# A float32 decoder trunk on one core: the high and the low moving part side by side in one 512-wide matmul, and outer weight sums made by adding transfers

## The chip, the cores and the metric

The kernel runs on one core of a Trainium2 chip. The metric is the device time of one execution in microseconds (us), with all inputs in the chip's main memory at the start and the output there at the end. Five engines work side by side, each through its own list of instructions, and wait for each other through semaphores: TensorE (PE, matmuls; its weight loads are listed as PEld), VectorE (DVE), ScalarE (ACT), GpSimd (POOL), and SyncE (SP), which issues most transfers.

## The reference

Two layers act on x of 512 tokens by 1024 features. Each layer is a feed-forward block, a token mixer (gated linear attention in layer 0, causal window means in layer 1), a cross-attention to a memory of 256 tokens, and a second feed-forward block. All is float32. What matters here are the four feed-forward blocks:

```python
def swiglu_ffn(h, w_gu, w_down):
    g, u = jnp.split(h @ w_gu, 2, axis=-1)
    return (jax.nn.silu(g) * u) @ w_down

for i in range(DEPTH):                                   # DEPTH = 2
    x = x + 0.5 * swiglu_ffn(rmsnorm(x, n_ffn1[i]), ffn1_w_gu[i], ffn1_w_down[i])
    ...                                                  # mixer, cross-attention
    x = x + 0.5 * swiglu_ffn(rmsnorm(x, n_ffn2[i]), ffn2_w_gu[i], ffn2_w_down[i])
```

`w_gu` is 1024 by 5632 (gate and up columns, 2816 each), `w_down` is 2816 by 1024.

## The kernel before

**Split numbers.** A float32 operand is split into a high and a low part. ACT writes the high part (`hi_part`, a copy to fp32r, L1388), DVE the low part (`lo_part`, value minus high part, L2055). One product then takes three matmuls: weights high times moving high, weights high times moving low, weights low times moving high. In the plain stages these are L418 to L420, 512 tokens wide.

**Slots and runs.** Gate and up are computed in 22 column blocks of 128 for each feed-forward block n = 0 to 3. The first 4, 2, 2 and 2 blocks are plain. The other 78 are "mixed slots". They come in eight runs, named (n, part): part 0 has 7, 9, 9 and 9 slots, part 1 has 11 each. Behind each run comes half of the down projection (`half_down`, or `down_by_token` for n = 3), with its own weights in the same buffers.

**A mixed slot** computes a 2 by 2 block product with seven products in place of eight. The weights of a slot have four quarters (first or second 512 rows; gate or up), the moving side has four as well (first or second 512 features; "low" tokens 0 to 255 or "high" tokens 256 to 511). PE makes the products in the order P1, P5, P6, P4, P2, P7, P3 (`mixed_slot`, L1013), where P4 still belongs to the slot before. Some use a quarter as it is, others a sum of quarters. Each product is four blocks of 128 rows by three 256-wide matmuls (`block_product`, L1000, matmuls at L1007 to L1009), 84 matmuls in a slot. P1 and P2 go to PSUM bank 6, P5 to bank 7, P6, P7 and P4 to one of two banks that alternate from slot to slot, P3 to bank d.

**Sums of weights.** DVE makes four sums for the next slot: two "outer" ones in one instruction (`sum_columns`, L2087, 1024 elements in each partition), and two more (`sum_three`, L2091; `sum_four`, L2101). Then each of the seven weight operands ("forms") is split by ACT (`form_hi`) and DVE (`form_lo`). A form may be written only when the product that used its buffer in the running slot is done.

**Behind the products.** ACT copies P1 from bank 6 into the alternating bank (L1487; its semaphore step is SEEDED, and PE's P6 waits for it), so that P6, P7 and P4 add to it. It moves P5 to SBUF (`sq`). DVE forms the fourth start value in bank d (`seed_fourth`, L2164), and then gate times norm, silu (ACT) and gate times up, for low and high tokens (L2172 to L2196, each 256 wide). Last come the split of the result (`half_hi` by ACT, `half_lo` by DVE).

**What sets the order.** The order on each engine is written out by hand in the three functions `mixed_run` (ACT, L1448; DVE, L2153) and `mixed_slot` (PE). An engine executes its list in order, so what stands behind a waiting instruction waits as well. In the run (3, 0) DVE also transposes a block of x in each slot (`turn_block`, L2427).

**Transfers.** SP loads each slot's weights in two transfers of 512 KB (`load_ffn`, L521), two slots ahead of use. POOL adds squares and issues a few transfers of its own.

Of the kernel before, what the change touches and what calls it, by code (L numbers as in the profile page):

```python
# [41 lines left out]
def trunk(nc, io, out):  # L42
# [153 lines left out]
    with ctx:  # L196
# [74 lines left out]
        s_hi, s_lo = region("s_hi", 0, [P, 4, KH, TH], F32R), region("s_lo", 16 * KB, [P, 4, KH, TH], F32R)  # L271
        w_sums = region("w_sums", 32 * KB, [P, 4, KH, P])
# [86 lines left out]
        names = """first_loaded first_cols_done vec_loaded gates_loaded identity_ready consts_ready mask_ready  # L359
# [14 lines left out]
                y_gained y_out_by_dve y_out_by_act stored  # L374
# [4 lines left out]
                mixed_act_step mixed_dve_step x_half_ready"""  # L379
# [106 lines left out]
        def _(sp):  # L486
# [33 lines left out]

            def load_ffn(n):  # L521
# [2540 lines left out]
```

## Time and profile before

| | us |
|---|---|
| median of 3 runs (1935.63 to 1936.52) | 1935.84 |
| the profiled execution, its own time | 1936.11 |
| its span, from the first to the last instruction | 1934.4 |
| PE busy | 1925.1 |
| DVE busy | 1410.6 |
| ACT busy | 964.2 |
| mean granted TensorE clock | 0.999 |

Spans and busy times come from the one profiled execution. A busy time counts an instruction from its start to its modelled end. Instructions of one engine overlap by their ends, so the distance between two starts tells how long one really holds its engine. The profiled execution took 1.7 us more than its span.

### The profile page before, as it was taken

The numbers are of one execution on the slowest core, as the hardware profiler recorded it, in microseconds if no ns is written. First come the engines' busy times: TensorE is split into PE (matmuls) and PEld (weight loads), VectorE is DVE, ScalarE is ACT, GpSimd is POOL, SyncE is SP. The second block draws the span as 40 slices with busy tenths as digits, with TensorE's granted clock in tenths as the row PEclk, the third lists the DMA queues.
The fourth block names the chain that finished last, engine by engine and source line by source line (L and its number), as shares of the span: only waits on it lengthen the run. The fifth ranks groups of instructions, "written<-read, shape, count | busy, mean of one in ns | idle before, by whom it ended". The sixth has DMA issues, their size and how long they took to land.

```text
span 1934.4 us, 31412 instructions
## 1 busy us (share of the span) xinstructions
PE 1925.1 (100%) x12020; PEld 1741.1 (90%) x12020; DVE 1410.6 (73%) x2173; ACT 964.2 (50%) x1612; POOL 168.6 (9%) x207
## 2 busy tenths in 40 slices
PE   9999999999999999999999999999999999999998
PEld 7998998888898889989998998999888889989997
DVE  7865985687765659947976995698487569937964
ACT  7542554355554546524644653355356446524543
POOL 2000002100112120000001000000312121200000
PEclk9999999999999999999999999999999999999999
DMA  6333334323433634333334333333353424343332
GB/s 181 87 104 103 109 93 136 108 66 109 131 127 114 174 87 110 103 103 109 101 91 120 91 100 94 101 109 104 112 180 116 109 74 116 109 159 109 109 98 87
DMA packets 285894, 215.01 MB, mean 111 GB/s; under 512 B 15347, under 2 KB 268401, under 8 KB 285793
## 3 DMA queue, kind: packets, MB, share of 16 engines
q1 hardware_dynamic: 270112, 192.96, 33.5%
q0 software_dynamic: 6752, 18.68, 3.7%
q10 hardware_dynamic: 8928, 2.11, 0.5%
q8 instruction: 54, 0.88, 0.2%
q14 instruction: 48, 0.39, 0.1%
HBM read 203.23 MB, written 10.49 MB: 110 GB/s over the span
## 4 chain that ended last, share of the span: by engine, by line
PE 96%; DVE 2%; ACT 1%; issue 1%; POOL 0%; DMA 0%; ACTq 0%; DVEq 0%; POOLq 0%
PE ps L418 18%; PE ps L420 18%; PE ps L419 18%; PE ps L1007 13%; PE ps L1009 13%; PE ps L1008 13%; DVE w_lo L2055 1%; ACT w_hi L1388 1%; POOL mem_scratch L721 0%; PE ps L933 0%; PE ps L867 0%; DVE sums L2808 0%; DMA x_tok<-in_x 0%; DVE sums L2828 0%; DVE up L2997 0%
## 5 line engine op out<-in xcount | busy, mean ns | idle before, releaser
L2055 DVE TENSOR_TENSOR w_lo<-raw,w_hi 128x512 fp32r<-128x512 f32 (+5 forms) x367 | 403.2, 1099 | 258.0 <-ACT w_hi L1388 257.3
L1388 ACT ACTIVATE w_hi<-raw 128x512 fp32r<-128x512 f32 (+5 forms) x367 | 341.5, 948 | 267.1 <-PE ps L420 254.9
L1007 PE MATMUL ps<-s_hi,w_hi 128*128 128x256 f32 x1248 | 353.8, 283 | 0.1
L1009 PE MATMUL ps<-s_hi,w_lo 128*128 128x256 f32 x1248 | 353.2, 283 | 0.0
L1008 PE MATMUL ps<-s_lo,w_hi 128*128 128x256 f32 x1248 | 353.2, 283 | 0.0
L1008 PE MATMUL ps<-h_lo,w_hi 128*128 128x256 f32 x936 | 264.9, 283 | 0.0
L1009 PE MATMUL ps<-h_hi,w_lo 128*128 128x256 f32 x936 | 264.9, 283 | 0.0
L1007 PE MATMUL ps<-h_hi,w_hi 128*128 128x256 f32 x936 | 264.8, 283 | 0.0
L1388 ACT ACTIVATE w_hi<-w_sums 128x512 fp32r<-128x512 f32 x312 | 187.5, 625 | 138.4 <-DVE w_sums L2087 69.4
L1007 PEld LDWEIGHTS ps<-s_hi,w_hi 128*128 128x128 f32 x1248 | 239.5, 192 | 0.9 <-issue 0.5
L1009 PEld LDWEIGHTS ps<-s_hi,w_lo 128*128 128x128 f32 x1248 | 239.5, 192 | 0.0
L1008 PEld LDWEIGHTS ps<-s_lo,w_hi 128*128 128x128 f32 x1248 | 239.5, 192 | 0.0
L2055 DVE TENSOR_TENSOR w_lo<-w_sums,w_hi 128x512 fp32r<-128x512 f32 x312 | 211.4, 681 | 0.0
L418 PE MATMUL ps<-half_hi,w_hi 128*128 128x512 f32 x528 | 205.7, 390 | 0.6 <-DVE w_lo L2055 0.6
L419 PE MATMUL ps<-half_lo,w_hi 128*128 128x512 f32 x528 | 205.5, 389 | 0.0
L420 PE MATMUL ps<-half_hi,w_lo 128*128 128x512 f32 x528 | 205.4, 389 | 0.0
L418 PE MATMUL ps<-h_hi,w_hi 128*128 128x512 f32 (+1 forms) x480 | 182.0, 379 | 0.5 <-DVE w_lo L2055 0.5
L419 PE MATMUL ps<-h_lo,w_hi 128*128 128x512 f32 (+1 forms) x480 | 180.2, 375 | 0.0
L420 PE MATMUL ps<-h_hi,w_lo 128*128 128x512 f32 (+1 forms) x480 | 180.1, 375 | 0.0
L1008 PEld LDWEIGHTS ps<-h_lo,w_hi 128*128 128x128 f32 x936 | 179.6, 192 | 0.3
L1007 PEld LDWEIGHTS ps<-h_hi,w_hi 128*128 128x128 f32 x936 | 179.6, 192 | 0.3
L1009 PEld LDWEIGHTS ps<-h_hi,w_lo 128*128 128x128 f32 x936 | 179.6, 192 | 0.0
(396 smaller groups left out, 3438.1 us busy)
## 6 DMA issues: line engine op xcount, KB each, us to landing
raw<-in_ffn_w_gu SPq DMA_DIRECT2D x172, 512.0 KB, 5.0
raw<-in_ffn_w_down SPq DMA_DIRECT2D x36, 768.0 KB, 4.4
raw<-in_x_w_kv SPq DMA_DIRECT2D x16, 1024.0 KB, 5.8
raw<-in_ffn_w_down SPq DMA_DIRECT2D x24, 640.0 KB, 4.2
raw<-in_gla_w_in SPq DMA_DIRECT2D x12, 1024.0 KB, 5.2
raw<-in_x_w_q SPq DMA_DIRECT2D x8, 1024.0 KB, 5.1
raw<-in_x_w_o SPq DMA_DIRECT2D x8, 1024.0 KB, 6.0
raw<-in_gla_w_out SPq DMA_DIRECT2D x8, 512.0 KB, 3.4
```

The source lines that it names most:

```text
L418: nc.tensor.matmul(out_ap, left[0], right[0], start=first, stop=False)
L419: nc.tensor.matmul(out_ap, left[0], right[1], start=False, stop=False)
L420: return nc.tensor.matmul(out_ap, left[1], right[0], start=False, stop=last)
L1007: nc.tensor.matmul(to, hi[:, kk, :], right_hi, start=fresh, stop=False, skip_group_check=True)
L1008: nc.tensor.matmul(to, hi[:, kk, :], right_lo, start=False, stop=False, skip_group_check=True)
L1009: last = nc.tensor.matmul(to, lo[:, kk, :], right_hi, start=False, stop=kk == KH - 1, skip_group_check=True)
L1388: return nc.scalar.activation(out_ap, in_ap, ACT.Copy, **kw)
L2055: return nc.vector.tensor_tensor(out_ap, value, hi.bitcast(F32), ALU.subtract)
```

## The change

**Moving parts side by side.** `h_hi` and `h_lo` become the two halves of `h_both`, `s_hi` and `s_lo` those of `s_both`. In six of the seven products (all but P5) one 512-wide matmul takes the high and the low part together: its left 256 columns of PSUM hold weights high times moving high, its right 256 columns weights high times moving low. The third matmul (weights low times moving high) adds to the left half as before. So a product has 8 matmuls in place of 12, and its value is the sum of the two halves of its bank. Adding these halves is new work of ACT (`up_right`, `high_right`, `low_right` take right halves to SBUF, a copy with scale -1 carries one to bank d, and the copy of P1 is 512 wide) and of DVE (`up_sum`, `high_sum`, `low_sum`, `up_part` with `up_ready`).

**Outer sums by transfer.** From the third slot of each run on (62 of the 78 slots) SP loads one quarter for each outer sum (256 KB each) two slots ahead. POOL then issues a transfer that adds the other quarter onto it (`accum_op=ALU.add`). DVE's `sum_columns` is then only a wait. The signs of sums on both sides are changed so that an addition serves.

**Cut diff** (the rest of it renames counters and semaphores):

```diff
@@ SP
+            def load_outer(m, both, s):
+
+                before, sums = 16 * transfers_before(m), outer_sums[in_run[m] % 2]
+                for g, (loaded_sem, opened, last_form) in enumerate(((sig.t1_loaded, OPENED, P5),
+                                                                     (sig.t3_loaded, 0, P7))):
+                    sp.wait_ge(*form_lo_count(m - 2, last_form))
+                    sp.wait_ge(loaded_sem, opened + before)
+                    sp.dma_start(sums[:, g], both[:, 0:KH, g, s * P:(s + 1) * P]).then_inc(loaded_sem, 16)
...
+                        if w in mixed_slots and by_transfer(mixed_slots.index(w)):
+                            load_outer(mixed_slots.index(w), both, s)
+                            sp.wait_ge(sig.w_lo_ready, w - 1)
+                            sp.dma_start(raw[:, w % 2, :, 0:P], both[:, :, 0, s * P:(s + 1) * P])\
+                              .then_inc(raw_loaded[w % 2], 16)
+                            sp.dma_start(raw[:, w % 2, KH:, P:], both[:, KH:, 1, s * P:(s + 1) * P])\
+                              .then_inc(raw_loaded[w % 2], 16)
+                            continue
@@ POOL
+            def add_outer(n, part, l):
...
+                pool.wait_ge(sig.t1_loaded, OPENED + before + 16)
+                pool.wait_ge(sig.t1_added, T1_OPENED + before)
+                pool.dma_start(sums[:, 0], up[:, 0:KH, s * P:(s + 1) * P], accum_op=ALU.add).then_inc(sig.t1_added, 16)
@@ PE, block_product
-                    nc.tensor.matmul(to, hi[:, kk, :], right_hi, start=fresh, stop=False, skip_group_check=True)
-                    nc.tensor.matmul(to, hi[:, kk, :], right_lo, start=False, stop=False, skip_group_check=True)
-                    last = nc.tensor.matmul(to, lo[:, kk, :], right_hi, start=False, stop=kk == KH - 1,
+                    if i == P5:
+                        nc.tensor.matmul(to, hi[:, kk, :], right[:, 0, :], start=fresh, stop=False, skip_group_check=True)
+                        nc.tensor.matmul(to, hi[:, kk, :], right[:, 1, :], start=False, stop=False, skip_group_check=True)
+                    else:
+                        nc.tensor.matmul(ps[:, bank, :], hi[:, kk, :], right, start=fresh, stop=False,
+                                         skip_group_check=True)
+                    last = nc.tensor.matmul(to, lo[:, kk, :], right[:, 0, :], start=False, stop=kk == KH - 1,
@@ PE, last_block (P4 of a run's last slot)
-                pe.wait_ge(sig.mixed_dve_step, dve_step(end - 1, C22_READY))
+                pe.wait_ge(sig.mixed_dve_step, dve_step(end - 1, UP_READY))
@@ ACT, mixed_run
+                def up_right(m, s):
+                    act.wait_ge(sig.product_done, product_count(m, P3))
+                    act.wait_ge(sig.mixed_dve_step, dve_step(m, UP_READY))
+                    hi_part(sq[:, s % 2, TH:], ps[:, d, TH:]).then_inc(sig.mixed_act_step, 1)
...
+                    if l > 0:
+                        up_right(m - 1, s - 1)
+                        form_hi(m, P3, sig.product_done, product_count(m - 1, P3))
                     act.wait_ge(sig.product_done, product_count(m, P1))
...
-                    nc.scalar.activation(ps[:, banks[l % 2], 0:TH], ps[:, 6, 0:TH], ACT.Copy).then_inc(sig.mixed_act_step, 1)
-                    if l > 0:
-                        form_hi(m, P3, sig.product_done, product_count(m - 1, P3))
+                    nc.scalar.activation(ps[:, banks[l % 2], :], ps[:, 6, :], ACT.Copy).then_inc(sig.mixed_act_step, 1)
@@ DVE, mixed_run, the slots after the first
+                    up_sum(m - 1, s - 1)
+                    form_lo(m, P3)
+                    low_gated(m - 1, s - 1)
...
+                    high_sum(m - 1, s - 1, before)
                     form_lo(m, P4)
...
+                    high_rms(m - 1, s - 1)
+                    low_sum(m, s)
                     if following:
                         sum_four(m + 1)
...
+                    low_rms(m, s)
+                    high_gated(m - 1, s - 1)
                     if following:
                         form_lo(m + 1, P2)
...
+                    up_part(m, s, b)
+                    half_mid_lo(s - 1)
+                    up_ready(m, s, b)
+                    if following:
                         form_lo(m + 1, P7)
```

**ACT where one slot ends and the next begins**, in the middle of a run. In the rows, `sq<-ps 128x256` behind the P7 form is `up_right` (new), `w_hi<-raw` is the form of P3 and then that of P1, and `ps<-ps` is the copy of P1 for which PE's P6 waits. Before:

```order
L1388 ACTIVATE half_hi<-t 128x512 [waits mixed_dve_step]
L1388 ACTIVATE w_hi<-w_sums 128x512 [waits product_done,w_sum_ready]
L1487 ACTIVATE ps<-ps 128x256 [waits mixed_dve_step,product_done]
L1388 ACTIVATE w_hi<-raw 128x512 [waits product_done,raw_loaded_even]
L1388 ACTIVATE w_hi<-raw 128x512 [waits product_done,raw_loaded_odd]
L1388 ACTIVATE sq<-ps 128x256 [waits mixed_dve_step,product_done]
```

The same place, of the changed kernel:

```order
L1464 ACTIVATE half_hi<-t 128x512 [waits mixed_dve_step]
L1464 ACTIVATE w_hi<-outer_odd 128x512 [waits product_done,t3_added]
L1464 ACTIVATE sq<-ps 128x256 [waits mixed_dve_step,product_done]
L1464 ACTIVATE w_hi<-raw 128x512 [waits product_done,raw_loaded_odd]
L1586 ACTIVATE ps<-ps 128x512 [waits mixed_dve_step,product_done]
L1464 ACTIVATE w_hi<-raw 128x512 [waits product_done,raw_loaded_even]
L1464 ACTIVATE sq<-ps 128x256 [waits mixed_dve_step,product_done]
```

Two instructions now stand ahead of the copy `ps<-ps`: `up_right`, which waits for a step of DVE, and the form of P3, which stood behind it.

**DVE in the second half of a slot**, in the middle of a run, from the form of P4 to the last sum with bank d. L2179 (before) forms the up value of the high tokens, for which PE's P4 waits. Before:

```order
L2055 TENSOR_TENSOR w_lo<-w_sums,w_hi 128x512 [waits form_hi_ready]
L2196 TENSOR_TENSOR t<-t,sq 128x256 [waits mixed_dve_step,silu_done]
L2101 TENSOR_TENSOR w_sums<-raw,w_sums 128x512 [waits form_lo_ready,w_sum_ready]
L2172 TENSOR_TENSOR t<-ps,rms 128x256 [waits mid_ready,product_done]
L2055 TENSOR_TENSOR w_lo<-raw,w_hi 128x512 [waits form_hi_ready]
L2055 TENSOR_TENSOR half_lo<-t,half_hi 128x512 [waits mid_hi_ready]
L2179 TENSOR_TENSOR sq<-ps,sq 128x256 [waits mixed_dve_step,product_done]
```

The same place, of the changed kernel (L2297 `high_rms`, L2302 `low_sum`, L2214 `sum_four`, L2307 `low_rms`, L2313 `high_gated`, L2320 `up_part`, L2325 `up_ready`):

```order
L2163 TENSOR_TENSOR w_lo<-inner_sums,w_hi 128x512 [waits form_hi_ready]
L2297 TENSOR_TENSOR t<-t,rms 128x256 [waits mixed_dve_step]
L2302 TENSOR_TENSOR t<-t,ps 128x256 [waits mixed_act_step]
L2214 TENSOR_TENSOR inner_sums<-raw,inner_sums 128x512 [waits form_lo_ready,w_sum_ready]
L2307 TENSOR_TENSOR t<-t,rms 128x256 [waits mixed_dve_step]
L2313 TENSOR_TENSOR t<-t,sq 128x256 [waits mixed_dve_step,silu_done]
L2163 TENSOR_TENSOR w_lo<-raw,w_hi 128x512 [waits form_hi_ready]
L2320 SCALAR_TENSOR_TENSOR sq<-ps,sq 128x256 [waits mixed_dve_step,product_done]
L2163 TENSOR_TENSOR half_lo<-t,half_hi 128x512 [waits mid_hi_ready]
L2325 TENSOR_TENSOR sq<-sq,ps 128x256 [waits mixed_dve_step]
```

`up_ready` (L2325), for which ACT's `up_right` and PE's P4 wait, stands ten instructions behind the form of P4 and last.

**DVE in a run's last slot**, from the split of the down weights (1536 elements, L2055 or L2163) on. Before:

```order
L2055 TENSOR_TENSOR w_lo<-raw,w_hi 128x1536 [waits w_hi_ready]
L2190 TENSOR_TENSOR t<-ps,rms 128x256 [waits product_done]
L2055 TENSOR_TENSOR w_lo<-w_sums,w_hi 128x512 [waits form_hi_ready]
L2196 TENSOR_TENSOR t<-t,sq 128x256 [waits mixed_dve_step,silu_done]
L2172 TENSOR_TENSOR t<-ps,rms 128x256 [waits mid_ready,product_done]
L2179 TENSOR_TENSOR sq<-ps,sq 128x256 [waits mixed_dve_step,product_done]
L2055 TENSOR_TENSOR half_lo<-t,half_hi 128x512 [waits mid_hi_ready]
```

And of the changed kernel:

```order
L2163 TENSOR_TENSOR w_lo<-raw,w_hi 128x1536 [waits w_hi_ready]
L2292 TENSOR_TENSOR t<-t,ps 128x256 [waits mixed_act_step]
L2163 TENSOR_TENSOR w_lo<-inner_sums,w_hi 128x512 [waits form_hi_ready]
L2297 TENSOR_TENSOR t<-t,rms 128x256 [waits mixed_dve_step]
L2302 TENSOR_TENSOR t<-t,ps 128x256 [waits mixed_act_step]
L2307 TENSOR_TENSOR t<-t,rms 128x256 [waits mixed_dve_step]
L2313 TENSOR_TENSOR t<-t,sq 128x256 [waits mixed_dve_step,silu_done]
L2320 SCALAR_TENSOR_TENSOR sq<-ps,sq 128x256 [waits mixed_dve_step,product_done]
L2163 TENSOR_TENSOR half_lo<-t,half_hi 128x512 [waits mid_hi_ready]
L2325 TENSOR_TENSOR sq<-sq,ps 128x256 [waits mixed_dve_step]
```

The step for which the run's last P4 waits (L2179 before, L2325 now) moved from ahead of `half_lo` to behind it, and four more instructions stand in between.

## Rows read from the trace of the kernel before

**Rows 1.** The page: busy time by engine, then the chain that ended last.
```profile
PE 1925.1 (100%) x12020; PEld 1741.1 (90%) x12020; DVE 1410.6 (73%) x2173; ACT 964.2 (50%) x1612; POOL 168.6 (9%) x207
...
PE 96%; DVE 2%; ACT 1%; issue 1%; POOL 0%; DMA 0%; ACTq 0%; DVEq 0%; POOLq 0%
```

**Rows 2.** Groups by form: count, busy us, mean ns of one, idle before.
```profile
L2087 DVE TENSOR_TENSOR w_sums<-raw 128x1024 f32<-128x1024 f32 x78 | 98.3, 1260 | 0.0
...
L1487 ACT ACTIVATE ps<-ps 128x256 f32<-128x256 f32 x78 | 28.7, 368 | 62.9 <-PE ps L1009 62.9
...
L1388 ACT ACTIVATE xq_hi<-ps 128x512 fp32r<-128x512 f32 x16 | 9.6, 597 | 32.5 <-PE ps L420 32.4
```

**Rows 3.** Timeline, PE, 512-wide matmuls (start us, length us): 39 starts apart.
```profile
20.05 0.39 PE L420 MATMUL ps<-h_hi,w_lo 128*128 128x512 f32 x1
...
28.89 0.39 PE L420 MATMUL ps<-h_hi,w_lo 128*128 128x512 f32 x1
```

**Rows 4.** Timeline, ACT, one slot from copy of P1 to the next.
```profile
94.58 0.37 ACT L1487 ACTIVATE ps<-ps 128x256 f32<-128x256 f32 x1 [0.88 <-PE ps L1009]
...
104.66 0.37 ACT L1487 ACTIVATE ps<-ps 128x256 f32<-128x256 f32 x1 [0.88 <-PE ps L1009]
104.94 1.14 ACT L1388 ACTIVATE w_hi<-raw 128x512 fp32r<-128x512 f32 x2
```

**Rows 5.** Timeline, DVE, the middle of the same slot; in brackets, idle before.
```profile
103.28 0.69 DVE L2055 TENSOR_TENSOR half_lo<-t,half_hi 128x512 fp32r<-128x512 f32 x1 [0.41 <-ACT half_hi L1388]
103.89 0.41 DVE L2179 TENSOR_TENSOR sq<-ps,sq 128x256 f32<-128x256 f32 x1
104.23 0.68 DVE L2055 TENSOR_TENSOR w_lo<-w_sums,w_hi 128x512 fp32r<-128x512 f32 x1
104.83 0.41 DVE L2185 TENSOR_TENSOR t<-t,ps 128x256 f32<-128x256 f32 x1
105.59 0.69 DVE L2055 TENSOR_TENSOR w_lo<-raw,w_hi 128x512 fp32r<-128x512 f32 x1 [0.35 <-ACT w_hi L1388]
106.20 1.22 DVE L2087 TENSOR_TENSOR w_sums<-raw 128x1024 f32<-128x1024 f32 x1
107.34 0.69 DVE L2055 TENSOR_TENSOR w_lo<-raw,w_hi 128x512 fp32r<-128x512 f32 x1
```

**Rows 6.** Timelines, PE and DVE, where the run (0, 1) begins.
```profile
184.59 0.28 PE L1007 MATMUL ps<-h_hi,w_hi 128*128 128x256 f32 x1
...
187.34 1.22 DVE L2087 TENSOR_TENSOR w_sums<-raw 128x1024 f32<-128x1024 f32 x1
```

**Rows 7.** Timelines, ACT, DVE and PE, where the run (0, 1) ends.
```profile
288.52 1.49 ACT L1388 ACTIVATE w_hi<-raw 128x1536 fp32r<-128x1536 f32 x1 [1.11 <-PE ps L1009]
...
290.04 1.76 DVE L2055 TENSOR_TENSOR w_lo<-raw,w_hi 128x1536 fp32r<-128x1536 f32 x1 [1.14 <-ACT w_hi L1388]
291.72 0.42 DVE L2190 TENSOR_TENSOR t<-ps,rms 128x256 f32<-128x256 f32 x1
...
295.47 0.40 PE L418 MATMUL ps<-half_hi,w_hi 128*128 128x512 f32 x1
```

**Rows 8.** Timelines, run (3, 0): copies of P1, and P7 behind DVE's L2164.
```profile
1626.55 0.37 ACT L1487 ACTIVATE ps<-ps 128x256 f32<-128x256 f32 x1 [0.36 <-PE ps L1009]
...
1631.71 0.42 DVE L2164 TENSOR_TENSOR ps<-ps,sq 128x256 f32<-128x256 f32 x1
...
1632.25 0.19 PEld L1007 LDWEIGHTS ps<-s_hi,w_hi 128*128 128x128 f32 x1 [0.19 <-issue]
...
1632.47 0.28 PE L1008 MATMUL ps<-s_lo,w_hi 128*128 128x256 f32 x1
...
1687.97 0.37 ACT L1487 ACTIVATE ps<-ps 128x256 f32<-128x256 f32 x1 [0.38 <-PE ps L1009]
```

**Rows 9.** One slot by window: busy by engine, clock, DMA share, GB/s; then DMA issues.
```profile
82.30:92.38 10.08, 10.08 (x86) 10.08 (x86) 9.33 (x18) 6.00 (x13) 0.00 (x0) 1.00 0.38 104
...
p_tok<-p_scratch POOLq DMA_DIRECT2D x12, 256.0 KB, 3.5
```

More of the change, by code:

```diff
@@ L183, in mixed_end, with by_transfer, transfers_before, sum_count @@
         return mixed_first[n, part] + mixed_count(n, part)
+    def by_transfer(m):
+        return in_run[m] >= 2
+    def transfers_before(m):
+        return sum(by_transfer(i) for i in range(m))
+    def sum_count(m, step):
+        return OPENED + 3 * m - transfers_before(m) + step - int(by_transfer(m))
     def first_of_run(m):
@@ L723, in memory_store, with add_run @@
                             .then_inc(sig.mem_stored, 16)
+            def add_outer(n, part, l):
+                m, s = mixed_first[n, part] + l, l + (PLAIN_FIRST[n], HALF)[part]
+                before, sums = 16 * transfers_before(m), outer_sums[l % 2]
+                up = (io.ffn1_w_gu, io.ffn2_w_gu)[n % 2][n // 2].rearrange("(k p) (g n) -> p k g n", p=P, g=2)[:, :, 1, :]
+                pool.wait_ge(sig.t1_loaded, OPENED + before + 16)
+                pool.wait_ge(sig.t1_added, T1_OPENED + before)
+                pool.dma_start(sums[:, 0], up[:, 0:KH, s * P:(s + 1) * P], accum_op=ALU.add).then_inc(sig.t1_added, 16)
+                pool.wait_ge(sig.t3_loaded, before + 16)
+                pool.wait_ge(sig.t3_added, T3_OPENED + before)
+                pool.dma_start(sums[:, 1], up[:, KH:, s * P:(s + 1) * P], accum_op=ALU.add).then_inc(sig.t3_added, 16)
+            def add_run(n, part):
+                for l in range(2, mixed_count(n, part)):
+                    add_outer(n, part, l)
             row = 0
@@ L1407, in form_hi @@
                 w = mixed_slots[m]
-                if i in SUM_OF:
-                    act.wait_ge(sig.w_sum_ready, OPENED + 3 * m + SUM_STEP[i])
+                if i == P5 and by_transfer(m):
+                    act.wait_ge(sig.t1_added, T1_OPENED + 16 * (transfers_before(m) + 1))
+                elif i == P7 and by_transfer(m):
+                    act.wait_ge(sig.t3_added, T3_OPENED + 16 * (transfers_before(m) + 1))
+                elif i in SUM_OF:
+                    act.wait_ge(sig.w_sum_ready, sum_count(m, SUM_STEP[i]))
                 else:
@@ L1503, in mixed_run @@
                     else:
+                        high_right(m - 1, s - 1, banks[(l + 1) % 2])
                         form_hi(m, P4, sig.product_done, product_count(m, P4))
+                    low_right(m, s)
+                    if l > 0:
                         high_silu(m - 1, s - 1)
@@ L1515, in mixed_run @@
                         form_hi(m + 1, P7, sig.product_done, product_count(m, P7))
+                up_right(m, s)
                 split_hi((w + 1) % 2, area[w + 1], loaded[w + 1], product_count(m, P3), slot_rows[w + 1],
                          sig.product_done)
+                high_right(m, s, banks[(end - m0 - 1) % 2])
                 high_silu(m, s)
@@ new lines, in high_rms, with low_sum @@
+                def high_rms(m, s):
+                    dve.wait_ge(sig.mixed_dve_step, dve_step(m, HIGH_SUM))
+                    nc.vector.tensor_tensor(t[:, s % 2, TH:], t[:, s % 2, TH:], rms[:, TH:], ALU.mult)\
+                      .then_inc(sig.mixed_dve_step, 1)
+                def low_sum(m, s):
+                    dve.wait_ge(sig.mixed_act_step, act_step(m, LOW_RIGHT))
+                    nc.vector.tensor_tensor(t[:, s % 2, 0:TH], t[:, s % 2, 0:TH], ps[:, 6, 0:TH], ALU.add)\
+                      .then_inc(sig.mixed_dve_step, 1)
```

263 lines of the change are left out of this document (159 added, 104 removed).

## The prediction

> **What bounds the kernel now.** I read the page first: PE is busy for 1925.1 of 1934.4 us and is 96% of the chain that ended last [rows 1]. DVE, at 73%, looks free, but that share is a mean over stages, so I read one mixed slot by window and by timeline. There DVE is busy for 9.33 of 10.08 us [rows 9]. Its list waits in two places only, 0.41 us for ACT's `half_hi` and 0.35 us for the form of P3 [rows 5]. A slot lasts from one copy of P1 to the next, 104.66 - 94.58 = 10.08 us [rows 4], which is 84 matmuls of 0.120 us without a hole. So in a mixed slot PE is the bound and DVE is 0.8 us behind it. In the run (3, 0), where DVE has one more instruction in each slot, the distance is already (1687.97 - 1626.55) / 6 = 10.24 us, and P7 there sits behind DVE's L2164 [rows 8]. DVE is the next bound, and it is near.
>
> **Matmuls.** Thirty-nine starts of 512-wide matmuls span 28.89 - 20.05 = 8.84 us, 0.2267 us each [rows 3]. Two 256-wide ones cost 0.240 us [rows 4]. One in place of two saves 0.0133 us. There are 6 x 4 = 24 such pairs in a slot, and 78 slots [rows 2]: 1872 x 0.0133 = **25.0 us** less on PE. A slot of PE alone becomes 24 x (0.2267 + 0.120) + 12 x 0.120 = 9.76 us. No row shows a 512-wide matmul next to a 256-wide one; the saving lies between 0 and 0.0267 us a pair (0.240 less 512 columns at 2.4 GHz, 0.2133, the granted clock being 1.00 [rows 9]), and I take the rows' 0.0133. The Trainium skill, "TensorE: Matmul & The Clock Gate", section "Back-to-back issue gap", gives an isolated warm gap of N / 2.4 + 2.5 ns, so one matmul fewer would save 2.5 ns and the whole change 4.7 us. The rows show 13.3 ns over the columns at both widths, so here the measurement decides.
>
> **DVE's sum.** Distances between starts give 0.60 us for 512 elements, 0.335 for 256, 1.14 for the outer sums [rows 5]. Before, a slot holds 10 of 512, one outer sum and 6 of 256: 6.03 + 1.14 + 2.01 = 9.18 us. After, the outer sum goes (-1.14) and four more of 256 come (+1.34): 9.38 us of 9.76. It still fits, but with half the slack. ACT gets three to four more PSUM reads of 0.28 us, well inside its idle time (6.00 busy of 10.08 [rows 9]). So no engine is full, and the question is who waits for whom.
>
> **The new wait.** PE's P6 needs the copy of P1 (SEEDED). Before, that copy needed P1 alone: it ended 0.03 + 0.16 + 0.37 = 0.56 us behind P1 [rows 4], while P5 keeps PE busy for 1.44, so P6 had 0.9 us in hand. Now ACT must first do `up_right` of the slot before, which waits for DVE's `up_ready`, and then the form of P3. `up_ready` is the last of ten DVE instructions that start with the form of P4, and they wait for PE's P4. This is a closed round, from one end of P4 to the next:
> - PE to ACT 0.03, `high_right` 0.285, form of P4 0.62 to its end, ACT to DVE 0.03: 0.965 us;
> - DVE: form of P4, `sum_four`, form of P2, `half_lo` at 0.603, five of 256 at 0.335, and `up_ready` 0.416 to its end [rows 5]: 4.50;
> - DVE to ACT 0.03, `up_right` 0.285 (104.94 - 104.66 [rows 4]), form of P3 0.52 (two take 1.14 to the end of the second [rows 4]), the copy 0.58: 1.415;
> - PE's restart, P6 and P4: 0.19 + 2 x 1.387 + 0.163 (a product's modelled end lies that far behind its last matmul's 0.120): 3.127.
>
> The sum is **10.005 us**. PE alone would need 9.76, so each steady slot holds PE for 0.245 us. Two of these prices have no row of their own. The copy, 512 wide in PSUM, lies between 0.37 (the 256-wide one) and 0.74 (twice that); a 512-wide PSUM read takes 0.597 [rows 2], so 0.58. PE's restart: L2164 ended at 1632.13, the weights were loaded from 1632.25, and the second matmul started at 1632.47, as if the product had begun at 1632.35 [rows 8]: 0.22. The best case is 0.03, as between ACT and DVE; I take 0.19.
>
> **First slot of a run (8).** DVE begins its list 187.34 - 184.59 = 2.75 us behind PE [rows 6] and must still make an outer sum itself, since transfers begin with the third slot. Walking on: outer sum done 3.96, `seed_fourth` at 4.92 (behind ACT's scaled copy of P6), forms of P1 and P5 and `sum_three`, ACT's forms of P6 and P4, then `low_right`, and DVE's `low_sum` at 8.01. From there 0.603 x 4 + 0.335 x 3 + 0.416 = 3.83 us to the end of `up_ready`, 11.84; + 1.42 for ACT and 0.19 for the restart = 13.45. PE could start the second slot's P6 at 11.44. Wait: **2.0 us**. Before, P1 of the second slot follows without a hole; now it also waits 0.24 us for `low_sum`.
>
> **Last slot (8).** P4 of the last slot now waits for `up_ready` behind DVE's split of the down weights and behind `half_lo`. From the slot's start: P6 ends at 4.62 (with its 0.245 hold), + 0.03, scaled copy 0.285, ACT's split 1.49, + 0.03 = 6.46; DVE's split 1.67 (291.72 - 290.04 [rows 7]), form of P4 0.603, six of 256 at 0.335 with one gap of 0.11 = 10.85; `half_lo` waits for ACT until 11.27; + 0.60 + 0.416 = 12.29; restart 12.48. PE is free at 10.0. Wait: **2.48 us**. Before, P4 ran through and down began at 295.47 without a hole [rows 7]. Down has all its inputs in time afterwards: its fifth weight block comes only 8.2 us in.
>
> **The sum.** 8 x 0.24 + 8 x 2.0 + 62 x 0.245 + 8 x 2.48 = 1.9 + 16.0 + 15.2 + 19.8 = 52.9 us of holes, + 0.6 for the third slot of the run (3, 0), where the transposes stand in the way, - 25.0 of matmuls, - 1.6 of the holes that this run has already. That is **+26.9 us**. The profiled execution took 1936.1 us, 0.3 above the median: **1963 us**.
>
> **At no cost:** the loads and the adding transfers. A load starts when DVE has split the same form two slots back, and its sum is split some 17 us later (two slots less the forms between). The load of 256 KB takes about 3.5 us [rows 9]; no adding transfer is in the trace, so I bound it by 3.5 and three times that. In the worse case 3 us are left. POOL is idle in the runs, and its later work (squares) starts after them. If the cover fails: rival 3.
>
> **Rivals.**
> 1. *PE stays the bound* (faster). The round would have to close in 9.76 us and the ends of a run without a hole; the former needs the copy at 0.37, the latter 4 us less of DVE work. With all holes gone: 1936.1 - 25.0 - 1.6 = 1910 us. Against it: the lists of DVE and ACT. At the favourable ends together (copy 0.37, pairs saving 0.0267) the same walk still gives +8 us, 1944.
> 2. *Holes and gain cancel* (within 0.2%): the holes at half, 26 us.
> 3. *Adds come late.* A slot now moves 1.8 MB in place of 1.0. With the DMA share 0.38 at 104 GB/s [rows 9] that is 0.66 of the slot if an add costs a load, 0.84 at twice, and the bound from three times on. At four times a slot takes 12.3 us, 2.3 more in each of 62: 1963 + 143 = 2106 us. Nothing speaks for it but the lack of a row.
> 4. *DVE or ACT slower by 5%*, from the doubled traffic or from PSUM reads beside 512-wide writes: each round grows by 0.25 us, 1979 us.
> 5. *The clock falls after the holes.* All stretches read 1.00 [rows 9], but none has such holes. Sixteen holes of 2 us, each followed by 2 us of work at 1.2 GHz in place of 2.4: + 16 us, 1979 us.
>
> **How the numbers follow.** Forecast 0.68 (1944 to 1978, by copy, restart and pair price); rivals: 1 has 0.08, 2 has 0.05, 3 has 0.05, 4 has 0.08, 5 has 0.06. The range 1944 to 1988 holds the forecast and rivals 4 and 5, 0.82. A measurement of this kernel can tell about 0.2%, 4 us, from no change: faster 0.08, same 0.05, slower 0.87.
>
> **What would show it.** Right: matmul starts 0.227 and 0.120 us apart in pairs; PE idle before P6 of each slot, released by ACT's copy, 0.2 to 0.3 us in the middle of runs and 2 us in the second slot; 2.5 us ahead of each run's last P4, released by DVE's L2325; copies of P1 10.0 us apart. Wrong: no idle time of PE before P6, or copies 9.8 us apart (rival 1); ACT or DVE waiting for t1_added or t3_added (3); DVE's 512-wide distance above 0.61 us (4); a granted clock below 0.99 (5).

## The result

The changed kernel takes 1989.5 us (median of 4 runs, 1981.5 to 1992.1) beside 1936.0 for the kernel before (4 runs, 1935.6 to 1936.5): ratio 1.0269, 95% interval 1.0255 to 1.0283. The forecast was 1963, its range 1944 to 1988. The direction was right; the loss is +53.5 us where +27 were forecast. The profiled execution took 1989.0 us, with a span of 1987.3 (1936.1 and 1934.4 before).

The page of the changed kernel, the lines that answer to [rows 1]: busy time by engine, the chain that ended last, and the adding transfers (count, KB each, median us from issue to landing).

```profile
PE 1944.0 (98%) x10148; PEld 1657.3 (83%) x10148; DVE 1456.4 (73%) x2423; ACT 1073.3 (54%) x1924; POOL 328.9 (17%) x331
...
PE 84%; DVE 9%; ACT 4%; issue 3%; DMA 0%; ACTq 0%; DVEq 0%
...
outer_even<-in_ffn_w_gu POOLq DMA_DIRECT2D x70, 256.0 KB, 4.8
```

PE has 1872 matmuls fewer and is busy 19 us longer. Its share of the chain fell from 96 to 84%. The two largest waits of PE (total us, times, longest):

```profile
PE ps L1083 <- DVE sq L2325: 17.7, 8, 2.3
PE ps L1083 <- ACT ps L1586: 15.9, 8, 2.1
```

Eight waits of 2.2 to 2.3 us for `up_ready` at the ends of the runs and eight of 2.0 to 2.1 for the copy of P1 in the second slots: both are the forecast's. But they are 33.6 us, not the whole loss. The rest is in what follows them. This is PE where the second slot of the run (0, 0) has its hole (timeline), then the same stretch and the next by window (PE busy first, then PEld, DVE, ACT, POOL; the granted clock is the third number from the end).

```profile
65.15 0.28 PE L1085 MATMUL ps<-s_both,w_lo 128*128 128x256 f32 x1
67.42 0.50 PE L1083 MATMUL ps<-s_both,w_hi 128*128 128x512 f32 x1 [1.99 <-ACT ps L1586]
67.75 0.28 PE L1085 MATMUL ps<-s_both,w_lo 128*128 128x256 f32 x1
...
68.22 0.61 PE L1083 MATMUL ps<-s_both,w_hi 128*128 128x512 f32 x1
68.63 0.41 PE L1085 MATMUL ps<-s_both,w_lo 128*128 128x256 f32 x1
68.84 0.63 PE L1083 MATMUL ps<-s_both,w_hi 128*128 128x512 f32 x1
...
71.75 0.28 PE L1085 MATMUL ps<-h_both,w_lo 128*128 128x256 f32 x1
71.86 0.40 PE L1083 MATMUL ps<-h_both,w_hi 128*128 128x512 f32 x1
```

```profile
66.00:68.00 2.00, 0.58 (x3) 0.54 (x4) 2.00 (x5) 2.00 (x5) 0.18 (x1) 1.00 0.51 60
68.00:70.00 2.00, 2.00 (x9) 1.66 (x8) 2.00 (x5) 0.98 (x3) 0.00 (x0) 0.56 1.01 200
70.00:72.00 2.00, 2.00 (x9) 1.77 (x8) 1.25 (x3) 0.63 (x2) 0.87 (x1) 0.59 1.10 314
72.00:74.00 2.00, 2.00 (x14) 1.72 (x13) 1.42 (x4) 1.29 (x3) 0.40 (x1) 1.00 1.15 252
```

From 68.2 to 71.7 a 512-wide matmul takes some 0.43 us to the next start and a 256-wide one 0.21, about twice the usual 0.23 and 0.12. The granted clock fell from 1.00 to 0.50 (2.4 to 1.2 GHz) 0.8 us after PE had begun again. Read in half microseconds it stays there for 3.41 us, which loses 1.71 us. Eleven of the sixteen holes have such a fall behind them: four second slots and seven run ends. None is in the trace of before while PE still has work.

To see where the 52.9 us between the two profiled executions lie I summed the starts of the first P5 matmul of each slot, over the eight runs:

| us | before | changed | difference | forecast |
|---|---|---|---|---|
| first P1 of the runs | 11.5 | 11.2 | -0.3 | -0.4 |
| first slots | 69.1 | 69.4 | +0.3 | -0.2 |
| second slots | 81.0 | 102.8 | +21.8 | +13.4 |
| the 54 slots between | 545.3 | 545.4 | +0.2 | -5.1 |
| last slots, to the start of down | 80.6 | 102.9 | +22.3 | +19.2 |
| all outside the runs | 1146.9 | 1155.5 | +8.6 | 0 |

The forecast's column is its own terms divided up (26.9 in all; its +0.6 and -1.6 for the run (3, 0) stand with the slots between). The +8.6 is mostly the end falls that reach into down: a run's last P4 lasts 1.4 us, the slow stretch 3.4. In e1_filled below, which has no fall, this row is 1146.8 again.

### The profile page after: what moved, and what is told of

Read it like the earlier page. It is cut to its first block, busy times and chain, and to the rows that moved or that the text cites. A ratio compares the mean times of both kernels' runs of the same rounds, so it can differ in the third digit from the quotient of the medians.

```text
span 1987.3 us, 28928 instructions
## 1 busy us (share of the span) xinstructions
PE 1944.0 (98%) x10148; PEld 1657.3 (83%) x10148; DVE 1456.4 (73%) x2423; ACT 1073.3 (54%) x1924; POOL 328.9 (17%) x331
## 4 chain that ended last, share of the span: by engine, by line
PE 84%; DVE 9%; ACT 4%; issue 3%; DMA 0%; ACTq 0%; DVEq 0%
PE ps L1083 19%; PE ps L442 17%; PE ps L443 16%; PE ps L444 16%; PE ps L1085 11%; DVE w_lo L2163 3%; ACT w_hi L1464 2%; PE ps L1081 2%; PE ps L1080 2%; DVE s_both L2163 0%; DVE half_lo L2163 0%; DVE outer_odd L2197 0%; DVE t L2302 0%; DMA raw<-in_x_w_kv 0%; DVE t L2307 0%
## 5 line engine op out<-in xcount | busy, mean ns | idle before, releaser
L2163 DVE TENSOR_TENSOR w_lo<-raw,w_hi 128x512 fp32r<-128x512 f32 (+5 forms) x367 | 402.9, 1098 | 254.7 <-ACT w_hi L1464 245.3
L1083 PE MATMUL ps<-s_both,w_hi 128*128 128x512 f32 x936 | 346.5, 408 | 16.4 <-ACT ps L1586 15.9
L1083 PE MATMUL ps<-h_both,w_hi 128*128 128x512 f32 x936 | 343.7, 404 | 17.7 <-DVE sq L2325 17.7
L1085 PE MATMUL ps<-s_both,w_lo 128*128 128x256 f32 x1248 | 352.2, 282 | 0.0
L1085 PE MATMUL ps<-h_both,w_lo 128*128 128x256 f32 x936 | 265.5, 284 | 0.0
L1085 PEld LDWEIGHTS ps<-s_both,w_lo 128*128 128x128 f32 x1248 | 237.3, 190 | 0.0
L1083 PEld LDWEIGHTS ps<-h_both,w_hi 128*128 128x128 f32 x936 | 178.6, 191 | 64.8 <-issue 20.0
L1083 PEld LDWEIGHTS ps<-s_both,w_hi 128*128 128x128 f32 x936 | 176.7, 189 | 66.7 <-ACT ps L1586 20.5
L442 PE MATMUL ps<-h_both,w_hi 128*128 128x512 f32 (+1 forms) x480 | 182.0, 379 | 0.8 <-DVE w_lo L2163 0.8
L443 PE MATMUL ps<-h_both,w_hi 128*128 128x512 f32 (+1 forms) x480 | 180.2, 375 | 0.0
L444 PE MATMUL ps<-h_both,w_lo 128*128 128x512 f32 (+1 forms) x480 | 180.1, 375 | 0.0
L1085 PEld LDWEIGHTS ps<-h_both,w_lo 128*128 128x128 f32 x936 | 179.6, 192 | 0.3
L2163 DVE TENSOR_TENSOR w_lo<-inner_sums,w_hi 128x512 fp32r<-128x512 f32 x156 | 107.0, 686 | 6.2
L442 PEld LDWEIGHTS ps<-h_both,w_hi 128*128 128x128 f32 x480 | 90.4, 188 | 16.8 <-DVE w_lo L2163 1.2
```

The source lines that it names most:

```text
L442: nc.tensor.matmul(out_ap, left[0], right[0], start=first, stop=False)
L443: nc.tensor.matmul(out_ap, left[0], right[1], start=False, stop=False)
L444: return nc.tensor.matmul(out_ap, left[1], right[0], start=False, stop=last)
L1083: nc.tensor.matmul(ps[:, bank, :], hi[:, kk, :], right, start=fresh, stop=False, skip_group_check=True)
L1085: last = nc.tensor.matmul(to, lo[:, kk, :], right[:, 0, :], start=False, stop=kk == KH - 1, skip_group_check=True)
L2163: return nc.vector.tensor_tensor(out_ap, value, hi.bitcast(F32), ALU.subtract)
```

## The steady slot, term by term

One round of ACT and DVE in the steady state (timelines, ACT and DVE, then PE), for [rows 4, 5]:

```profile
92.26 0.38 ACT L1464 ACTIVATE t<-ps 128x256 f32<-128x256 f32 x1 [0.50 <-PE ps L1085]
92.54 0.62 ACT L1464 ACTIVATE w_hi<-inner_sums 128x512 fp32r<-128x512 f32 x1
...
93.20 0.69 DVE L2163 TENSOR_TENSOR w_lo<-inner_sums,w_hi 128x512 fp32r<-128x512 f32 x1
...
97.28 0.41 DVE L2325 TENSOR_TENSOR sq<-sq,ps 128x256 f32<-128x256 f32 x1
...
97.79 0.39 ACT L1464 ACTIVATE sq<-ps 128x256 f32<-128x256 f32 x1 [0.77 <-DVE sq L2325]
98.07 0.62 ACT L1464 ACTIVATE w_hi<-raw 128x512 fp32r<-128x512 f32 x1
98.59 0.59 ACT L1586 ACTIVATE ps<-ps 128x512 f32<-128x512 f32 x1
...
99.23 0.51 PE L1083 MATMUL ps<-s_both,w_hi 128*128 128x512 f32 x1
99.58 0.28 PE L1085 MATMUL ps<-s_both,w_lo 128*128 128x256 f32 x1
```

From `high_right` to DVE's form of P4: 93.20 - 92.26 = 0.94 (forecast 0.935). DVE's list: 4.08 + 0.41 = 4.49 (4.50). The copy's end behind `up_right`'s start: 99.18 - 97.79 = 1.39 (1.385). Only DVE to ACT took 97.79 - 97.69 = 0.10 where 0.03 was put in, and the way from the copy's end to the next `high_right` 3.18 in place of 3.16. The round is 10.10 us instead of 10.005; the copies of P1 are 10.10 apart, those of before 10.08 [rows 4]. Little of the wait shows as idle time: P6 starts 0.20 us behind P5's last matmul (99.03 in the same timeline) where 0.12 is usual, and its first wide matmul holds PE for 99.58 - 99.23 = 0.35 us in place of 0.23. The two make up the 0.19 us by which a slot is longer than the 9.91 of PE alone (below).

## The experiments

The kernel before ran beside each group of experiments; its median was 1936.2 to 1936.4 us each time, so times of different groups can be compared. Three edits of order, A, B and C, come back in several kernels.

**Is it idle time that lets the clock fall?** The kernel e1_filled keeps every wait and gives PE something to do ahead of it:

```diff
+            def fill(n, part, times):
...
+                for _ in range(times):
+                    nc.tensor.matmul(ps[:, (o + 3) % 4, :], h_both[:, 0, 0, 0:P], h_both[:, :, 0, 0:TH], ...)
...
                 form_ready(P6)
+                if l == 1 and j is None:
+                    fill(n, part, 8)
                 pe.wait_ge(sig.mixed_act_step, ...)
```

(and `fill(n, part, 9)` ahead of the waits of `last_block`). The kernel also writes out the second and third slots of a run in PE's list instead of looping over them; no run has that alone.

> The changed kernel; before its wait for the copy of P1 in the second slot of each run TensorE does 8 extra 512-wide matmuls, and before its wait ahead of the run's last P4 it does 9 more, all into a PSUM bank that nobody reads (8 x 0.227 = 1.8 us of a hole of 2.13, 9 x 0.227 = 2.0 us of one of 2.35). The first two slots behind the first are written out instead of looped. The waits stay, so no hole closes; only TensorE is not idle in it. Theory (the clock falls because TensorE was idle, 11 times in the profiled execution of the changed kernel, 1.71 us lost each time): granted clock 0.999, no matmuls at 0.43 us spacing, time 1989.5 - 11 x 1.71 = 1971 us. Rival (the clock falls for another cause, the wide matmuls or the doubled traffic, and its place behind the holes is chance): clock 0.99 as before the fill, 1982 to 1992 us.

Measured: 1972.3 us (4 runs, 1971.9 to 1972.5), mean clock 1.0. PE and the windows in the same place:

```profile
65.54 0.28 PE L1085 MATMUL ps<-s_both,w_lo 128*128 128x256 f32 x1
65.66 2.00 PE L1093 MATMUL ps<-h_both 128*128 128x512 f32 x8
67.72 0.50 PE L1083 MATMUL ps<-s_both,w_hi 128*128 128x512 f32 x1
...
68.00:70.00 2.00, 2.00 (x13) 1.74 (x13) 2.00 (x5) 1.48 (x5) 0.00 (x0) 1.00 1.08 174
```

P6 starts 67.72 - 65.54 = 2.18 us behind P5's last matmul, nearly as long as the hole was (2.27), so the wait is all there; the granted clock is 1.00 from 7.4 us to behind PE's last matmul. More work in the same holes makes the kernel 17.2 us faster, ten falls' worth. The spread of the runs goes from 10.6 to 0.6 us: it was the falls that varied (of the changed kernel's runs the shortest, 1981.5 us, had a mean clock of 0.995, the longest, 1992.1, one of 0.988). The rival (wide matmuls or traffic) is out, since both are still there. They are so in e5_both_orders too, which has loops as the changed kernel has, no such holes, and no fall either.

> As e1_filled, with 4 extra matmuls ahead of each of the 16 waits in place of 8 and 9: 0.9 us of work, then 1.2 to 1.5 us idle. Theory (shorter idle stretches leave the clock alone, as the eight of 1.42 us in e3_ready_first did): granted clock 0.999, no matmuls at 0.43 us spacing, 1972 us as with the full fill, all runs within 1 us. Rival (any idle stretch of over a microsecond can let it fall): some falls, 1975 to 1985 us, runs some us apart.

Measured: 1973.6 us (1973.5 to 1973.9), no fall. The waits that are left:

```profile
PE ps L1083 <- DVE sq L2337: 10.5, 8, 1.4
PE ps L1083 <- ACT ps L1598: 8.4, 9, 1.1
```

With 1.0 to 1.4 us idle in place of 2.0 to 2.3, none of the 16 waits let the clock fall.

> The changed kernel once more, unaltered, for its clock falls. Theory (16 waits of 2.1 to 2.4 us lie where the clock can fall, and which of them it falls behind is not set by the program): 1.71 us each, another set of waits than the 11 of the first profile, runs spread over 1980 to 1993 us in line with their mean granted clocks. Rival (fixed places: the second slots of a layer's second part never, the others always): the same 11, 1989 us.

Measured: 1988.1 us (1986.5 to 1991.0). Again 11 falls, but another set: the holes ending at 1026.53 and 1124.76, whose counterparts had a fall in the first profile, have none, and those ending at 1816.78 and 1918.62 have one. Windows of two of them, behind the second slots of two runs:

```profile
1124.00:1126.00 2.00, 1.24 (x7) 1.11 (x8) 2.00 (x5) 2.00 (x5) 0.00 (x0) 1.00 1.11 147
1126.00:1128.00 2.00, 2.00 (x13) 1.72 (x12) 2.00 (x5) 1.16 (x4) 0.00 (x0) 1.00 0.80 210
...
1816.00:1818.00 2.00, 1.22 (x3) 1.04 (x4) 1.74 (x5) 2.00 (x5) 0.27 (x1) 0.66 0.36 90
1818.00:1820.00 2.00, 2.00 (x8) 1.70 (x7) 1.27 (x3) 0.32 (x2) 0.39 (x1) 0.50 1.30 201
```

The rival of fixed places is out. What decides which of the holes of 2.0 to 2.3 us lets the clock fall stays open. e8_no_transfers (below) has the same sixteen holes and six falls.

**B: the copy of P1 first.** It stands on ACT ahead of `up_right` and the form of P3:

```diff
-        ACT_ORDER = (UP_RIGHT, SEEDED, P5_TAKEN,
+        ACT_ORDER = (SEEDED, UP_RIGHT, P5_TAKEN,
...
-                    if l > 0:
-                        up_right(m - 1, s - 1)
-                        form_hi(m, P3, sig.product_done, product_count(m - 1, P3))
                     act.wait_ge(sig.product_done, product_count(m, P1))
...
                     nc.scalar.activation(ps[:, banks[l % 2], :], ps[:, 6, :], ACT.Copy).then_inc(sig.mixed_act_step, 1)
+                    if l > 0:
+                        up_right(m - 1, s - 1)
+                        form_hi(m, P3, sig.product_done, product_count(m - 1, P3))
```

> The changed kernel with one order changed on ScalarE: in each slot the 512-wide copy of P1 stands ahead of up_right and the form of P3 instead of behind them. Theory (the holes before P6 are this order): no idle time before P6; second slot 2.13 us shorter in 8 runs (-17.0) and 4 clock falls fewer (-6.8), 62 steady slots 9.91 us (24 pairs x 0.353 + 12 x 0.120) in place of 10.10 (-11.8); the waits ahead of the last P4 stay at about 2.35 us: 1989.5 - 35.6 = 1954 us. Rival (VectorE is then the bound, since up_right comes 0.5 us later and VectorE's up_sum waits for it): steady slots 10.0 to 10.2 us, VectorE's idle time in front of up_sum, 1960 to 1972 us.

Measured: 1961.0 us (1960.6 to 1962.9). Steady slots (ACT's copies of P1), then PE's waits:

```profile
85.46 0.58 ACT L1583 ACTIVATE ps<-ps 128x512 f32<-128x512 f32 x1 [0.25 <-PE ps L1085]
95.38 0.58 ACT L1583 ACTIVATE ps<-ps 128x512 f32<-128x512 f32 x1 [0.64 <-PE ps L1085]
...
PE ps L1083 <- DVE sq L2325: 17.5, 8, 2.2
PE ps L1083 <- DVE ps L2276: 6.1, 8, 1.4
```

No wait for the copy is left, and slots are 95.38 - 85.46 = 9.92 us with PE as the bound. It is 7 us above the expectation. The second slot found a new wait, P7 for DVE's `seed_fourth` (L2276), 6.1 us in all: VectorE comes late out of the first slot. Six falls, all at run ends.

**A: `up_ready` ahead of `half_lo`** on DVE, ACT as it was:

```diff
                     up_part(m, s, b)
-                    half_mid_lo(s - 1)
                     up_ready(m, s, b)
+                    half_mid_lo(s - 1)
```

> The changed kernel with one order changed on VectorE: up_ready ahead of half_lo (half_mid_lo) in every slot but the first, ScalarE's order as it was. Theory (the steady slot is the closed round P4, VectorE, ScalarE, P6, which loses half_lo's 0.60 us: 10.10 - 0.62 = 9.48, under the 9.91 of TensorE alone): steady slots 9.91 us, no wait before P6 (62 x 0.19 = -11.8), the second slot's wait unchanged at 1.97 us, the wait ahead of the last P4 shorter by 1.04, about 1.2 us (-8.3): 1989.5 - 20.1 = 1969 us, and down to 1957 if waits of 1.2 us leave the clock alone (7 falls less, -12.0). Rival (slots are 10.10 us for another cause, TensorE's own rate or the traffic): slots stay 10.10, 1981 us.

Measured: 1958.1 us (1957.9 to 1959.9). Copies 96.09 - 86.17 = 9.92 us apart, so the round was what held the slot at 10.10, not PE's rate or the traffic. The waits, and the clock behind the first run's end (a hole of 1.27 us up to 125.47):

```profile
PE ps L1083 <- ACT ps L1586: 16.0, 8, 2.1
PE ps L1083 <- DVE sq L2325: 10.1, 8, 1.3
...
125.47 0.47 PE L1083 MATMUL ps<-h_both,w_hi 128*128 128x512 f32 x1 [1.27 <-DVE sq L2325]
...
124.00:126.00 2.00, 0.73 (x5) 0.52 (x4) 1.97 (x6) 1.55 (x4) 0.00 (x0) 1.00 0.94 324
126.00:128.00 2.00, 2.00 (x12) 1.69 (x11) 1.26 (x2) 1.35 (x2) 0.00 (x0) 1.00 0.01 4
```

The end holes of 1.3 us had no fall, eight of eight; the second slots' 2.0 us had three.

**C: in the last slot the chain of P4 ahead of the split of the down weights:**

```diff
-                    if not following:
-                        split_hi(w % 2, area[w], ...)
                     if l == 0:
...
                     if l > 0:
                         high_silu(m - 1, s - 1)
+                    if not following:
+                        split_hi(w % 2, area[w], ...)
...
-                    else:
-                        split_lo(w % 2, area[w], w + 1, slot_rows[w])
                     high_sum(m - 1, s - 1, before)
...
-                    half_mid_lo(s - 1)
                     up_ready(m, s, b)
+                    if not following:
+                        split_lo(w % 2, area[w], w + 1, slot_rows[w])
```

(`half_mid_lo` stands behind the split in the last slot, and in its old place in the others.)

> The changed kernel with the last slot of each run in another order: ScalarE's split of the first down weights moves behind low_right and high_silu, VectorE's split of them and half_lo behind up_ready, so that the form of P4 and up_ready no longer stand behind them. Theory (the wait ahead of the last P4 is this order): it goes (-8 x 2.35 = -18.8) with 7 clock falls (-12.0), the second slot and the steady slots unchanged: 1959 us. Rival (the wait moves: down's first matmuls now wait for the split): 1 to 1.7 us of idle time at each start of down, released by VectorE's split, 1967 to 1985 us.

Measured: 1962.5 us (1961.3 to 1966.0). The end hole is gone and did not move to down's start: the last slots take 82.6 us in all (102.9 before the edit). Four falls behind second slots. `up_ready` now ends at 126.63, P4 follows P3 at 126.79 without a hole, and the split stands behind it (timelines of DVE and PE, cf. [rows 7]):

```profile
125.76 0.42 DVE L2320 SCALAR_TENSOR_TENSOR sq<-ps,sq 128x256 f32<-128x256 f32 x1
126.21 0.42 DVE L2325 TENSOR_TENSOR sq<-sq,ps 128x256 f32<-128x256 f32 x1
126.58 1.76 DVE L2163 TENSOR_TENSOR w_lo<-raw,w_hi 128x1536 fp32r<-128x1536 f32 x1
...
126.68 0.28 PE L1085 MATMUL ps<-s_both,w_lo 128*128 128x256 f32 x1
126.79 0.45 PE L1083 MATMUL ps<-h_both,w_hi 128*128 128x512 f32 x1
```

**Together.**

> The changed kernel with both edits of e2_copy_first and e4_last_p4_first together. Theory (all that the changed kernel lost are the waits of these two orders and the clock behind them): e2's 1961 us less 8 x 2.34 = 18.7 of waits and 6 x 1.71 = 10.3 of clock falls: 1932 us, granted clock 0.999, a little faster than the kernel before; 78 slots at 9.92 less the second slot's wait for VectorE's L2276 (0.9 us in five of the runs). Rival (something else is lost as well, since TensorE alone should come to 1936 - 13 = 1923): 1936 us or more.

> e5_both_orders with up_ready ahead of half_lo in every slot as in e3_ready_first. Theory (the round has its slack already by the copy's order, so this third edit has nothing to give): within 2 us of e5_both_orders, about 1932 us. Rival (VectorE's lateness in the second and third slots, the wait for L2276, comes from half_lo's place): the wait of 0.9 us goes in five runs, 4 to 5 us faster than e5.

Measured: e5 (B and C) 1935.1 us (11 runs, 1933.9 to 1936.2), ratio 0.9994 (0.9985 to 1.0003); e6 (A, B and C) 1936.0 us, ratio 0.9997 (0.9988 to 1.0006). Neither has a fall. Two orders take back 54.4 us, all of the loss. e5 is 3 us above its expectation; no run tells why. A adds nothing once B gives the round its slack: the wait for L2276 is still in e6. What is left of e5's waits, and L2276 in its first slot:

```profile
PE ps L1083 <- DVE ps L2276: 6.2, 8, 1.5
...
59.09 0.43 DVE L2276 SCALAR_TENSOR_TENSOR ps<-ps,sq 128x256 f32<-128x256 f32 x1 [1.50 <-ACT ps L1598]
```

In the first slot DVE idles for 1.50 us in front of that very instruction while two others that it could do stand behind it. Hence e9: in the first slot

```diff
-                        seed_fourth(m, s, b)
                         form_lo(m + 1, P1)
                         sum_three(m + 1)
+                        seed_fourth(m, s, b)
                         form_lo(m + 1, P5)
```

> e5_both_orders with one more order changed, on VectorE in the first slot of each run: the form of P1 and sum_three of the next slot ahead of seed_fourth (L2276), where VectorE now idles for 1.50 us until ScalarE's scaled copy. Theory (e5's second slots are 0.6 to 1.0 us long because VectorE comes out of the first slot that late): VectorE 1.2 us earlier, the wait for L2276 gone in the second slot, 8 x 0.5 to 0.9 us less: 1935 - 6 = 1929 us, about 0.35% under the kernel before. Rival (the second slot waits for something else in the row, the inner sums or ScalarE's forms, which do not move): 1933 to 1935 us.

Measured: 1927.0 us (5 runs, 1925.6 to 1928.8), ratio to the kernel before 0.9951 (0.9937 to 0.9964): 0.5% faster than it. DVE's idle time there is down to 0.29 and no wait for L2276 is left in the view of PE's waits. L2276 and two slots of the first run:

```profile
58.77 0.43 DVE L2276 SCALAR_TENSOR_TENSOR ps<-ps,sq 128x256 f32<-128x256 f32 x1 [0.29 <-ACT ps L1598]
...
73.95 0.58 ACT L1583 ACTIVATE ps<-ps 128x512 f32<-128x512 f32 x1 [0.44 <-PE ps L1085]
83.87 0.58 ACT L1583 ACTIVATE ps<-ps 128x512 f32<-128x512 f32 x1 [0.66 <-PE ps L1085]
```

**What one matmul fewer is worth.** e7 and e10 make each wide matmul as two narrow ones, all else kept:

```diff
-                        nc.tensor.matmul(ps[:, bank, :], hi[:, kk, :], right, start=fresh, stop=False, ...)
+                        nc.tensor.matmul(ps[:, bank, 0:TH], hi[:, kk, :], right[:, 0, :], start=fresh, stop=False, ...)
+                        nc.tensor.matmul(ps[:, bank, TH:], hi[:, kk, :], right[:, 1, :], start=False, stop=False, ...)
```

In e7 the second one has start=fresh too, and that kernel leaves out the first term of P1's left half. The Trainium skill, "PSUM — Partial Sum Buffer", section "Terms", states that a starting matmul clears the marks of what was written over the whole bank in which it writes. No trace can show this, and the number of matmuls is the same in e7 and e10.

> e5_both_orders with each of its 1872 512-wide matmuls of the six products made as two 256-wide ones into the two halves of the same bank: all orders, copies, sums and transfers of e5 kept. It prices one matmul fewer with TensorE as the bound. Theory (the pair costs 0.353 us with its single one where three narrow ones cost 0.360, as the slots of 9.92 us say): + 1872 x 0.007 = + 13 us, slots of 10.08 us. Rival 1 (the prediction's 0.0133 us a pair): + 25 us over e5. Rival 2 (the gap of 2.5 ns of the Trainium skill, "TensorE: Matmul & The Clock Gate", section "Back-to-back issue gap"): + 4.7 us.

> e9_first_slot with each 512-wide matmul made as two 256-wide ones, as in e7_narrow, but only the left one opens the bank, so that P1's first term is kept. TensorE is the bound in every slot now. Theory (0.0067 us a pair, by e7's slots of 10.08 beside 9.92): + 1872 x 0.0067 = + 12.5 us over e9_first_slot, 1941 us. Rivals as for e7_narrow: 0.0133 us a pair gives + 25, 0.0025 us gives + 4.7.

Measured: e7 1944.3 us, 9.2 over e5; e10 1937.3 us (1936.8 to 1938.0), 10.4 over e9. The copies in e10:

```profile
84.79 0.58 ACT L1585 ACTIVATE ps<-ps 128x512 f32<-128x512 f32 x1 [0.82 <-PE ps L1087]
94.87 0.58 ACT L1585 ACTIVATE ps<-ps 128x512 f32<-128x512 f32 x1 [0.82 <-PE ps L1087]
```

Slots of 10.08 beside 9.92: (10.08 - 9.92) / 24 = 0.0067 us a pair; over the whole kernel 10.4 / 1872 = 0.0056. Less than 0.0067 is gained in the run (3, 0), which DVE holds in part, and in the last slots (10.19 us in e9, 10.24 in e10, in most runs), and outside the runs e9 is 0.9 us longer. So the matmuls are worth 9 to 12 us. The forecast's 25.0 is twice that. The 4.7 us by the gap of 2.5 ns that the Trainium skill gives ("TensorE: Matmul & The Clock Gate", section "Back-to-back issue gap") is half of it.

**What the adding transfers are worth.**

```diff
     def by_transfer(m):
-        return in_run[m] >= 2
+        return False
...
             def add_outer(n, part, l):
+                return
```

> The changed kernel without the adding transfers: VectorE makes the outer sums in every slot as before, all loads as before; side-by-side matmuls, copy and orders as changed. Theory (the transfers free VectorE, which without them has 9.38 + 1.14 = 10.52 us of work in a slot and its waits on top): slots of 10.7 to 11.1 us, VectorE the bound, 62 x 0.6 to 1.0 more: 2027 to 2052 us, less some clock falls. Rival (the doubled traffic slows the engines, so without it they gain what VectorE pays): slots 10.1 to 10.5 us, 1990 to 2012 us.

Measured: 2020.0 us (2018.8 to 2021.3), 30.5 over the changed kernel. One slot by window, from copy to copy:

```profile
88.00:98.67 10.67, 10.17 (x62) 8.85 (x61) 10.57 (x22) 7.35 (x16) 0.00 (x0) 1.00 0.34 98
```

DVE is busy for 10.57 of 10.67 us; the 54 slots between take 577.8 us, 32.4 more, and five clock falls fewer take part of it back. So the transfers work as meant. The slots, 10.70 us on average, are at the low end of what was expected, and the five falls, 5 x 1.71 = 8.6 us, are about the 7 us by which 2020 lies below 2027. Their traffic costs nothing that these runs show.

## Why the prediction was off

**Matmuls, -25.0 us: mis-sized.** The step took 0.0133 us a pair from equal neighbours (512 beside 512, 256 beside 256). In the steady slots a wide matmul and its narrow one take 0.3533 us, not 0.3467: (9.92 - 1.44) / 24. Just behind holes, and in some slots, single pairs do take 0.347. The saving is 0.0067 (e7, e10), inside the range given and half the value taken. It mattered little to the changed kernel, where the round sets the slot; it halves what a mended kernel gains.

**DVE's sum: right.** It fits without the outer sums (e9: slots of 9.92 in seven of eight runs) and does not fit with them (e8).

**The new wait, 62 x 0.245: right in mechanism, the round 0.095 short.** 0.07 of it is the one handoff from `up_ready` to ACT, put at 0.03 from other rows and measured at 0.10. Slots of 10.10 in place of 10.005 are +5.9 us over 62. The wait itself is smaller than forecast (0.19) since PE alone needs 9.91 and not 9.76. A and B, each alone, prove the round: opened at either end it leaves slots of 9.92.

**First slot, 8 x 2.0, and last slot, 8 x 2.48: right.** Measured from start to start, less the usual 0.12, mostly 2.13 and 2.35 us of lost matmul time each, 17.2 and 18.9 us in all; the sum of the two is 36.1 where 35.8 was forecast. That it fits so well is in part luck, since one is 0.13 above its term and the other 0.13 below. The orders named there are the cause: B removes the one, C the other. Behind the first a smaller wait comes up, for L2276, which e9 removes. Rival 2, with half these holes, is out.

**The sum had no term for the clock.** This is the step that failed. Rival 5 had the mechanism (falls behind these 16 holes) at a chance of 0.06 and 1 us for each; it happened behind 11, at 1.71 us each, 18.8 us. The prediction saw that no stretch of before has such holes and took a granted clock of 1.00 to hold all the same. The sign that it set, a granted clock below 0.99, was too coarse: eleven falls leave a mean of 0.990 in the profiled execution. With the falls its +26.9 would have been +45.7. The round adds 54 x 0.095 = 5.1 in the slots between, the smaller saving up to 8 x 72 x 0.0067 = 3.8 in the others: +54.6 beside +52.9 measured. Without its falls the same sum gives +35.8, and e1_filled, which has none, came out at +36.2. So the 1.7 us seem to lie with the falls: the profiled executions of the two kernels differ by 1987.3 - 1970.7 = 16.6 us, not by 18.8. Why a fall costs a little less than it loses on the clock isn't shown. (A small error that hardly moves the sum: the run (3, 0) of before holds 1.3 us of holes where 1.6 was taken off.)

**Adding transfers at no cost: right.** They landed in 4.8 us, between the bounds of 3.5 and 10.5, and neither ACT nor DVE waits for them in the view of waits. Rival 3 is out, and so is rival 4: DVE's part of the round took 4.49 us where 4.50 was put. Rival 1 described e9, not this kernel: at 1927 us it is 17 above the 1910 that went by 25 us for the matmuls.

## What to carry over

When a change hands an engine's inputs to its helpers, look at the order in which they serve it: here two misplaced pieces of work cost 54 us, and the wide matmuls were worth 10. Price a hole on TensorE as its length plus what the clock does behind it; in this kernel a hole of 2.0 to 2.3 us costs up to 1.7 us more when the clock falls behind it, and one of 1.0 to 1.4 only itself. A wait that can't be removed can be covered by matmuls into a free bank, as in e1_filled.

## Unexpected on the chip

- Idle stretches of 2.0 to 2.3 us let the granted clock fall from 1.00 to 0.50 behind 11 of 16 (twice, different ones), 6 of 8 (e2's ends), 3 of 8 and 4 of 8 (the second slots of e3 and e4) and 6 of 16 (e8), 41 of 72 in all; stretches of 1.0 to 1.4 us behind none of 24 (e3's ends, e11). The slow stretch was 3.41 us long each time.
- A 512-wide matmul next to a 256-wide one has two rates, 0.353 and 0.347 us a pair, and keeps one for a whole slot. What sets it isn't known.
- The handoff from DVE to ACT took 0.10 us behind `up_ready` and 0.03 from `high_rms` to ACT's next silu in the same slot (94.23 to 94.26).
